# A 16-bit look-up of the picks, three gathered dots a head inside the ranking, and the first gates read back in three pieces

## The reference, cut to what matters

```python
def _peer(x, wq, subkeys, u, v):
    q = (xf @ wq).reshape(n, PEER_HEADS, 2, PEER_HALF)
    s = jnp.einsum('nhpd,hpkd->nhpk', q, subkeys).astype(jnp.float32)
    s_top, i_top = lax.top_k(s, PEER_TOPK)
    cand = s_top[:, :, 0, :, None] + s_top[:, :, 1, None, :]
    cand_idx = i_top[:, :, 0, :, None] * PEER_NKEYS + i_top[:, :, 1, None, :]
    best_s, best_j = lax.top_k(cand.reshape(n, PEER_HEADS, -1), PEER_TOPK)
    expert = jnp.take_along_axis(cand_idx.reshape(n, PEER_HEADS, -1), best_j, axis=-1)
    gate = jax.nn.softmax(best_s, axis=-1)
    ...
        h = jnp.einsum('nd,nhkd->nhk', xb, u[eb]).astype(jnp.float32)
        coef = (gb * jax.nn.gelu(h, approximate=False)).astype(xb.dtype)
        return jnp.einsum('nhk,nhkd->nd', coef, v[eb])
```

## Time and profile before

| | |
|---|---|
| median of 3 runs | 2049.67 us (2046.78 to 2054.2) |
| the profiled execution | 2070.54 us, of which its span is 2068.8 us |
| granted TensorE clock, mean over the span | 0.946 |
| PE busy | 1919.1 us, 93% |
| DVE busy | 1532.9 us, 74% |
| POOL busy | 609.5 us |

### The profile page before, as it was taken

One profiled execution on the slowest core, in us unless ns is written; L12 is line 12 of the kernel. 1 busy time (PEld: TensorE's weight loads), 2 busy tenths in 40 slices (PEclk: granted clock), 3 DMA queues, 4 the chain that ended last, 5 costly groups with the idle time before them and its releaser, 6 DMA issues.

```text
span 2068.8 us, 34098 instructions
## 1 busy us (share of the span) xinstructions
PE 1919.1 (93%) x13250; PEld 1627.3 (79%) x13250; DVE 1532.9 (74%) x2826; ACT 764.1 (37%) x1113; POOL 609.5 (29%) x403
## 2 busy tenths in 40 slices
PE   5989998888999879999999999969999999999996
PEld 4978876348983349999999999957887877889995
DVE  6277994314446248999989999958787868879898
ACT  3222454442220033334346666533333333333332
POOL 2322343000000015555552222252222323235550
PEclk9988999787999989999999999989999999999998
DMA  3211232001005024434468988899999999999991
GB/s 125 72 62 41 92 112 72 0 1 43 3 4 203 0 85 152 137 131 140 147 240 295 319 313 322 306 380 356 345 369 354 348 319 351 356 317 339 377 356 68
DMA packets 173720, 416.53 MB, mean 201 GB/s; under 512 B 13953, under 2 KB 89217, under 8 KB 170385
## 3 DMA queue, kind: packets, MB, share of 16 engines
q1 hardware_dynamic: 119728, 256.16, 36.1%
q0 software_dynamic: 36864, 134.23, 17.2%
q10 hardware_dynamic: 16992, 24.26, 3.2%
HBM read 363.08 MB, written 51.51 MB: 200 GB/s over the span
## 4 chain that ended last, share of the span: by engine, by line
PE 40%; DVE 14%; DMA 6%; issue 1%; ACT 0%; SPq 0%; DVEq 0%; ACTq 0%
PE ps L2012 21%; PE ps L1927 11%; PE ps L1931 5%; DMA gates<-dense_gates 3%; PE ps L1985 3%; DVE is_place L2099 2%; DMA coef<-parked_gelu 2%; DVE is_place L2094 1%; DMA w_staged<-in_stream 1%; DVE picks L2102 1%; DVE top_at L2060 1%; DVE top_at L2069 1%; DVE s_head L2063 1%; DVE best_at L2060 1%; DVE best_at L2069 1%
## 5 line engine op out<-in xcount | busy, mean ns | idle before, releaser
L2012 PE MATMUL ps<-w_hl,coef_hl 128*128 128x512 f32 x2304 | 539.7, 395 | 23.5 <-DVE coef_hl L2186 23.5
L2012 PEld LDWEIGHTS ps<-w_hl,coef_hl 128*128 128x128 f32 x2304 | 436.8, 190 | 119.6 <-DVE coef_hl L2186 25.6
L1927 PE MATMUL ps<-h_hl,w_hl 128*128 128x384 f32 (+1 forms) x2304 | 447.8, 346 | 15.6 <-DVE h_hl L2032 8.7
L1927 PEld LDWEIGHTS ps<-h_hl,w_hl 128*128 128x128 f32 x2304 | 406.9, 190 | 30.2 <-issue 9.1
L1542 POOL DMA_INDIRECT gathered_rows<-in_u_rows,pick_index x128 | 161.6, 1262 | 379.1 <-DVE pick_hidden L1552 359.4
L1861 ACT ACTIVATE w_hl<-w_staged 128x1024 fp32r<-128x1024 f32 x143 | 152.2, 1064 | 246.7 <-PE ps L2012 153.5
L1542 POOL DMA_INDIRECT gathered_rows<-in_v,pick_index x128 | 168.5, 1316 | 239.9 <-DVE h_tok L1561 201.6
L1931 PE MATMUL ps<-h_hl,w_hl 128*128 128x384 f32 (+1 forms) x1152 | 230.0, 340 | 0.0
L1931 PEld LDWEIGHTS ps<-h_hl,w_hl 128*128 128x128 f32 x1152 | 203.3, 188 | 5.0
L1801 POOL TENSOR_TENSOR w_hl<-w_staged,w_hl 128x1024 fp32r<-128x1024 f32 x64 | 164.4, 2571 | 136.4 <-ACT w_hl L1826 111.9
L1561 DVE SCALAR_TENSOR_TENSOR h_tok<-gathered_rows,pick_hidden,h_tok 128x1024 f32<-128x1024 f32 x128 | 164.1, 1282 | 6.7 <-DVE h_tok L1561 0.5
(11 more groups left out here) (315 smaller groups left out, 2558.0 us busy)
## 6 DMA issues: line engine op xcount, KB each, us to landing
w_staged<-in_stream SPq DMA_DIRECT2D x132, 512.0 KB
h1T<-in_v SPq DMA_DIRECT2D x66, 512.0 KB
w_staged<-in_v SPq DMA_DIRECT2D x62, 512.0 KB
dense_gates<-lot SPq DMA_DIRECT2D x24, 1024.0 KB
gates<-dense_gates SPq DMA_DIRECT2D x16, 1536.0 KB
w_staged<-in_w_in_t SPq DMA_DIRECT2D x40, 512.0 KB
parked_gelu<-h1T ACTq DMA_DIRECT2D x102, 192.0 KB
coef<-parked_gelu SPq DMA_DIRECT2D x102, 192.0 KB
```

Source lines behind the costliest of these rows:

```text
L1927: nc.tensor.matmul(ps[:, bank, 0:width], w_hl[:, j % RING, 0, P * k:P * (k + 1)], h_hl[:, part, k, lo:SEQ], start=(k == 0 and part == 0), ...
L2012: last = nc.tensor.matmul(ps[:, 2 + 2 * t + half, :], coef_hl[:, k % HLS, c, P * t:P * (t + 1)], w_hl[:, s % RING, v, 512 * half:512 * (ha ...
```

## The change

It has three parts. In `rank` the look-up of the picked keys (16 comparisons of 16, times the keys, summed) is done in bfloat16, in whole instructions over both key lists, and the sum over 16 places by halves instead of by one reduction. The index of a head's picks is ready at the end of its own `rank`; after it, DVE does three dots of the head before, and POOL issues three gathers behind the last low part of the next head's tiles, after a wait for that index. So 21 dots are in the ranking, 48 in the lots as before, and 6 (one a tile) in the tiles behind, where there were 18; 75 dots precede the sums where there were 66. `gates` for even eights of keys is a buffer of its own, `gates0`, and its first filling is read in three pieces: lots 0 to 15 after the store of lot 17, lots 16 to 21 after the store of lot 23, lots 22 and 23 where the whole was read.

```diff
+    FIRST_GATES = {LOTS - 7: slice(0, LOTS - 8), LOTS - 1: slice(LOTS - 8, LOTS - 2)}
+    FIRST_READS = len(FIRST_GATES) + 1
...
-    DOTS_A_LOT, DOTS_BEHIND = 2, 3
+    DOTS_A_HEAD, DOTS_A_LOT, DOTS_BEHIND = 3, 2, 1
+    IN_LOTS = DOTS_A_HEAD * (PEER_HEADS - 1)
...
+        gates0 = sb("gates0", [P, LOTS, LOOP * LOT])
...
+            def load_first_gates(lots):
+
+                for j in range(2):
+                    sp.wait_ge(lot_stored[j], 16 * (lots.stop // 2))
+                sp.dma_start(gates[0][:, lots], dense[lots, :, 0:LOOP * LOT].rearrange("l p k -> p l k")
+                             ).then_inc(gates_landed[0], 16)
...
                 sp.dma_start(dense[n], lot[:, n % 2, :, :].rearrange("p k n -> p (k n)")).then_inc(lot_stored[n % 2], 16)
+                if n in FIRST_GATES:
+                    load_first_gates(FIRST_GATES[n])
             load_from(FIRST_BEHIND + RING, QUERIES + PARKED)
-            for j in range(2):
-                sp.wait_ge(lot_stored[j], 16 * (LOTS // 2))
-            load_gates(0)
+            load_first_gates(slice(LOTS - 2, LOTS))
...
+            for s in range(BY_POOL):
+                low(s, s)
+                h, m = divmod(s - PER_HEAD, PER_HEAD)
+                if 0 <= h < PEER_HEADS - 1 and m == PER_HEAD - 1:
+                    pool.wait_ge(gathering["picked"], h + 1)
+                    for n in range(DOTS_A_HEAD * h, DOTS_A_HEAD * (h + 1)):
+                        gather_rows(nc, pool, a, gathering, n)
...
-                for x in range(2):
-                    put(v_.tensor_tensor(is_place[:, x], is_place[:, x],
-                                         keys[:, x].unsqueeze(2).broadcast_to([P, NT, K, K]), ALU.mult))
                 settle()
-                put(v_.tensor_reduce(picks[:, 0:2, :, bass.ds(i * (2 * K) + r * K, K)], is_place[:, :], AX.X, ALU.add))
+                put(v_.tensor_tensor(is_place[:, :].rearrange("p x j k t -> p (x j) k t"),
+                                     is_place[:, :].rearrange("p x j k t -> p (x j) k t"),
+                                     keys[:, :].rearrange("p x j t -> p (x j) t").unsqueeze(2).broadcast_to([P, 2 * K, K, NT]),
+                                     ALU.mult))
                 settle()
+                for half in (8, 4, 2):
+                    put(v_.tensor_tensor(by_place[:, :, 0:half], by_place[:, :, 0:half], by_place[:, :, half:2 * half], ALU.add))
+                    settle()
+                put(v_.tensor_tensor(picks[:, 0:2, :, K * h:K * (h + 1)],
+                                     is_place[:, :, 0].rearrange("p x k t -> p x t k"),
+                                     is_place[:, :, 1].rearrange("p x k t -> p x t k"), ALU.add))
                 settle()
+                v_.scalar_tensor_tensor(gathering["index"][:, now], picks[:, 0, 0, now], float(EXPERT_KEYS),
+                                        picks[:, 1, 0, now], ALU.mult, ALU.add).then_inc(gathering["picked"], 1)
+                for n in range(DOTS_A_HEAD * (h - 1), DOTS_A_HEAD * h):
+                    if n >= 0:
+                        dot_rows(nc, dve, h_tok, gathering, n)
```

More of the change, by code:

```diff
@@ L1599, in peer @@
     BEHIND = PARKED - (4 * PEER_HEADS + BETWEEN + 2 * LOTS)
-    DOTS_A_LOT, DOTS_BEHIND = 2, 3
-    used_behind = [DOTS_A_LOT * LOTS + DOTS_BEHIND * (n + 1) for n in range(BEHIND)]
+    DOTS_A_HEAD, DOTS_A_LOT, DOTS_BEHIND = 3, 2, 1
+    IN_LOTS = DOTS_A_HEAD * (PEER_HEADS - 1)
+    used_behind = [IN_LOTS + DOTS_A_LOT * LOTS + DOTS_BEHIND * (n + 1) for n in range(BEHIND)]
     EARLY = used_behind[-1]
@@ L1678, in peer @@
             cand = sb("cand", [P, NT, K * K], at=first)
-            is_place = sb("is_place", [P, 2, NT, K, K], at=first)
+            top = sb("top", [P, 2, NT, K], at=first)
+            top_at = sb("top_at", [P, 2, NT, K], U32, at=first)
+            best = sb("best6", [P, NT, K], at=first)
+            best_at = sb("best_at", [P, NT, K], U32, at=first)
+            split_at = sb("split_at", [P, 2, NT, K], U32, at=first)
+            keys = sb("keys", [P, 2, K, NT], BF16, at=first)
+            place = sb("place", [P, 2, K, NT], BF16, at=first)
+            count16 = sb("count16", [P, K, K, NT], BF16, at=first)
+            is_place = sb("is_place", [P, 2, K, K, NT], BF16, at=first)
         with ExitStack() as second:
@@ L1802, in low @@
                                         w_hl[:, j % RING, 0, :].bitcast(F32), ALU.subtract).then_inc(w_low, 1)
-            with pool.Fori(0, BY_POOL // 8) as i:
-                for j in range(8):
-                    low(i * 8 + j, j)
-            pool.wait_ge(gathering["picked"], 1)
-            for n in range(2 * PICKS):
+            for s in range(BY_POOL):
[5 more added lines that the diff above has]
+                        gather_rows(nc, pool, a, gathering, n)
+            pool.wait_ge(gathering["picked"], PEER_HEADS)
+            for n in range(IN_LOTS, 2 * PICKS):
                 gather_rows(nc, pool, a, gathering, n)
@@ L2078, in rank @@
                 dve.sem_inc(topped, 1)
-                put(v_.tensor_copy(keys[:, :], top_at[:, :]))
+                put(v_.tensor_copy(keys[:, :], top_at[:, :].rearrange("p x t k -> p x k t")))
                 put(v_.tensor_tensor(cand[:, :, :].rearrange("p t (x y) -> p t x y", x=K),
@@ L2097, in rank @@
+                by_place = is_place[:, :].rearrange("p x j k t -> p x j (k t)")
+                put(v_.tensor_tensor(by_place, place[:, :].rearrange("p x k t -> p x (k t)").unsqueeze(2).broadcast_to([P, 2, K, rows]),
+                                     count16[:, :, :, :].rearrange("p j k t -> p j (k t)").unsqueeze(1).broadcast_to([P, 2, K, rows]),
+                                     ALU.is_equal))
                 settle()
-                for x in range(2):
-                    put(v_.tensor_tensor(is_place[:, x], is_place[:, x],
-                                         keys[:, x].unsqueeze(2).broadcast_to([P, NT, K, K]), ALU.mult))
+                put(v_.tensor_tensor(is_place[:, :].rearrange("p x j k t -> p (x j) k t"),
+                                     is_place[:, :].rearrange("p x j k t -> p (x j) k t"),
+                                     keys[:, :].rearrange("p x j t -> p (x j) t").unsqueeze(2).broadcast_to([P, 2 * K, K, NT]),
+                                     ALU.mult))
@@ new lines, in rank @@
+                settle()
+                now = slice(K * h, K * (h + 1))
+                v_.scalar_tensor_tensor(gathering["index"][:, now], picks[:, 0, 0, now], float(EXPERT_KEYS),
[3 more added lines that the diff above has]
+                        dot_rows(nc, dve, h_tok, gathering, n)
+            for h in range(PEER_HEADS):
+                rank(h)
@@ L2165, in _ @@
                 low(BY_POOL + TILES_A_LOT * (n + 1))
-                for x in range(DOTS_A_LOT * n, DOTS_A_LOT * (n + 1)):
+                for x in range(IN_LOTS + DOTS_A_LOT * n, IN_LOTS + DOTS_A_LOT * (n + 1)):
                     dot_rows(nc, dve, h_tok, gathering, x)
@@ L2181, in weigh @@
                 at = LOT * (k % LOOP)
-                v_.tensor_tensor(x, x, gates[:, k // LOOP % 2, :, at:at + LOT], ALU.mult).then_inc(weighed, 1)
+                v_.tensor_tensor(x, x, gates[k // LOOP % 2][:, :, at:at + LOT], ALU.mult).then_inc(weighed, 1)
             def low_coef(k):
```

39 lines of the change are left out of this document (13 added, 26 removed).

## The result

| | median us | executions | ratio to before, 95% interval |
|---|---|---|---|
| before | 2052.24 | 10 | 1 |
| after | 2060.89 | 10 | 1.0039 [1.0021, 1.0056] |
| after, again, on another occasion | 2058.03 | 12 | 1.0045 [1.0025, 1.0066] |

The change costs 0.4%, some 8.6 us. 2029 was forecast, and this lies outside the range, on its slow side.

A forecast was written before the change was run, and what follows sets the result against it. PE, busy 93% of the span, bounds the kernel, so gains come from its idle or low-clock time. Terms -2.9 + 0.5 - 6.3 - 12.2 - 2.7 + 3 = -20.6 us; 2049.67 - 20.6 = 2029 us; range 2019 to 2043.

The forecast's parts named there:

- Ranking, -2.9: In the ranking: 16-bit look-up and POOL's wait make a head 30.6 us, so PE's 2.9 us wait at the picks goes.
- Just in time: In the ranking: head 6's index at 1003.2, gathers and low part end 1010.3, tile 48 wanted at 1010.38; PE loses nothing.
- (c): In the ranking: POOL's wait does not keep it off DVE's stretches; PE loses 27.9 us, 2057 us, slower; chance 0.06.
- (d): In the look-up: 16-bit is no faster than f32; 33.5 us a head, 2049 us, no change; chance 0.04.
- Rival (b): In the ranking: DVE lags, 31 to 33.5 us a head, tile 48 late; 2037 at 31.7, 2042 at 32.5; chance 0.13.
- Lots, +0.5: In the lots: 1 MB of gates, about 3 us of transfer before two tiles, costs PE 0.5 (0 to 3).
- Behind the lots, -6.3: Tiles behind the lots: twelve fewer gathers cut PE's 4.41 us wait to 1, matmuls after it at full clock: -6.3 us.
- The gap, -12.2: Before the sums: PE's 14.55 us wait becomes 2.4, as coef is issued behind only 128 KB of gates: -12.2 us.
- Clock and second pause, -2.7 and +3: Start of the sums: -2.7 us low-clock time regained; +3 (0 to 8) from a late v tile at key 1.
- rival (a): Before the sums: v tiles and second gates read jam, SP held again; gap returns half of 14.9, 2037 us; chance 0.15.
- The sums, 0: In the sums: same dots and additions for parked keys, nine fewer later beside a busy PE; change 0 us.
- The chance of 0.06 for slower: Whole kernel: probability of slower, all given to the rival where lost time on DVE grows beside POOL, 2057 us.

The follow-up runs named there:

- after again: The changed kernel run once more without an edit: 2058.03 us, 1.0045 of the kernel before.
- spread: Changed kernel with first gates read in eleven 128 KB pieces, every second lot behind the tile loads, the last 128 KB behind the lots: 2047.87 us, 0.9993.
- fills: Ten scratch-tile fills on DVE ahead of the first weighing: added to before, 2051.40 us, 1.0013; to the changed kernel without early pieces, 2047.61 us, 0.9990.
- big piece: Changed kernel with the 1 MB gates piece kept at lot 17 and the other 512 KB read whole behind the lots: 2053.48 us, 1.0010.

## Why the prediction was wrong, step by step

The times can be put together from ratios, as means of kernels that differ in one thing:

- **Look-up and dots** at the old place: 0.9949, 0.9984 and 0.9966 (mean 0.9966) against the 1.0009, 0.9996 and 1.0013 of before's structure (1.0006): -0.40%, **-8 us**.
- **Placement** 96 to 32: the same 0.9966 against 1.0004, 1.0007, 0.9990 and 0.9993 (0.9999): +0.33%, **+7 us**.
- **The pieces**: 1.0059 against 1.0006, 1.0017 against 0.9966, and 1.0042 (after and after again) against 0.9999: +0.53, +0.51, +0.43%, **+10 us**.

Their sum is +9 us, and +8.6 was measured. Each is uncertain by 3 us or so; spread reads and fills are counted as no pieces, since their ratios are no different, and 0.9949 rests on 6 executions.

**Ranking, -2.9.** Right in its mechanism, and still worth about nothing. The durations and the wait of POOL came as written, and a mean head of 30.3 us for my 30.6. "Just in time" was late: a `cand` of 3.42 us and a `keys` cast of 3.97 made the index of head 6 ready 208.7 us after the ranking's start, not 207.0, and the gathers with the low part took 8.1 us, not 7.1. PE waited 2.35 us for the 2.9 that went, with slow matmuls behind it. From tile 48 to tile 64 it took 71.8 us in both traces of after, and 70.7 or 72.3 in those of kernels with before's ranking. Rivals (c) and (d) did not happen. Rival (b) did in one trace, that of big piece, with heads of up to 34.1 us and 6.6 us of waits for POOL.

**Lots, +0.5.** Wrong, and the first of the two steps that failed. I took the transfer's length, 3 us, for its price, and wrote that "one tile of PE with its fours lasts longer". What counts is when the tiles behind it on SP's queue land: ACT waited 7.51 us. And I said that nothing shows a tile's slack; there was slack, by the trace one disturbance deep, and the `v` tiles five lots later needed it. PE lost 4.19 us and time in slow matmuls.

**Behind the lots, -6.3.** Wrong, in part for the same reason. I had the 384 KB "cost 1" and the wait fall to 1; it was 5.82 with slow matmuls behind it. Counted to the end of the last parked tile, after is at 620.3 us from the layer's first tile and before at 613.2 (first sum less its pause): +7 where -8.7 stood in the sum. But without the pieces it is 612.8. Even then the 6.3 were not there: waits of 1.8 and 2.0 us stayed.

**The gap, -12.2.** Right in size, 12.4. Its cause was half seen: the fewer gathers were enough for it, and the pieces added nothing to them.

**Clock and second pause, -2.7 and +3.** The 3.02 us are luck. The pause that I had costed, for a tile of `v` at the second key, did not come in after (1.37 us in after again), and the one that came is that of rival (a): the second read of `gates`, with SP held 11.91 us over a `coef`. In the other kernels with the new ranking it is 2.85 to 5.7 us, and gone in the one with the fills. Where one pause of 14.6 us stood, 5 to 10 us in two or three are left at the first keys (2.11 and 3.02; 2.11, 1.28 and 2.85; 3.17 and 5.28; 3.83 and 6.65). Little of the 2.7 came back: the first 90 matmuls took 22.82 us where the first 86 had taken 22.77, and the 12 behind the second pause took 5.49.

**The sums, 0.** The second step that failed. "Beside a PE that is busy throughout: 0" held for the waits, but each of the 2304 matmuls took 1.5% longer. It is the term that the sum did not have.

**The sum again, from the traces of before and after.** To the end of the last parked tile I had -8.7, and it was +7.1. From there to the 145th matmul of the sums, eight keys on, the gap, the clock and the second pause were to give -11.9, and gave -7.0 (50.4 to 43.4 us). There PE stands at 663.6 us in both kernels: what was lost ahead of the sums and what was won at their start are equal. The other 2160 matmuls take 3.4 ns more each, +7.3 where I had 0. That makes +7.4 for the -20.6 that was forecast, and +8.6 was measured.

**The base.** The profile of before was slow ahead of the change's part, so to put the difference on the median was right, and the pause ahead of the sums was 14.2 to 14.9 us in all five traces of kernels with before's ranking and its one read. But the last sum came between 1270.4 and 1280.6 us in four traces of kernels with before's structure. A difference under 10 us cannot be read off two traces; it took ratios of medians.

The chance of 0.06 for slower, given to one mechanism on POOL and DVE, left out the queue of tile loads that the change edits in plain sight.

## What to carry to other kernels

A transfer moved ahead of others on a queue can cost more than its own bytes (here 10 us for an estimate of 1.5), so look at which load lands next, and at how many disturbances the ring's slack still covers. Small reads behind the loads cost nothing here. Before costing a cure for a pause, ask what else was in the memory at that time; here taking gathers away shortened it, and moving the read only moved the wait. When a forecast number comes out, check that it is the same wait. When tiles are removed or added, compare the spacing of untouched instructions in both traces: 64 bytes cost as much as the change's useful half gave. The best version is the look-up and the dots with one whole read or spread reads and the 64 bytes back: 2042 us, 0.9949 [0.9932, 0.9967] in 6 executions and 0.9966 [0.9949, 0.9984] in 12, faster than both kernels.

## What the runs showed of the hardware

- At the same granted clock of 1.00, the sums' matmuls started every 232, 229 or 227 ns with `coef_hl` at 32, 96 or 160 bytes modulo 512. Moving only `coef_hl` and `coef` by 64 bytes gave the middle value.
- A DVE cast with one input, 128 elements of 32 bits, took 0.23 us alone (the kernel before). Beside POOL's low parts (2.4 us each) it ended 0.08 to 0.15 us behind one of them, in all 20 traces; where two stood back to back it got in between them or waited for both (3.97 us), and once for three (6.27 us, in spread).
- After a wait of 2.35 us in the ranking, PE's next 16 matmuls took 4.51 us where others take 2.93.
- PE reached the same instruction, after the same program, between 754.8 and 769.8 us in 20 executions.
